# Moving shifted weight slots and the mixers' region from 64 to 128 bytes off their partner's remainder modulo 256

## The reference

```python
def conv_ffn(h, w_up, conv_w, conv_b, w_down):
    u = causal_dwconv(h @ w_up, conv_w, conv_b)
    g, val = u[..., :D_FF], u[..., D_FF:]
    return (jax.nn.gelu(g, approximate=True) * val) @ w_down

for layer in range(DEPTH):
    h = rms_norm(x, norm_mix_pre[layer])
    m = even_mixer(h, ...) if layer % 2 == 0 else odd_mixer(h, ...)
    x = x + rms_norm(m, norm_mix_post[layer])
    h = rms_norm(x, norm_ffn_pre[layer])
    x = x + rms_norm(conv_ffn(h, ...), norm_ffn_post[layer])
```

## Time and profile before

| | us |
|---|---|
| median of the runs | 1075.27 |
| profiled execution, whole | 1075.82 |
| its span, first to last instruction | 1074.0 |
| TensorE busy | 1064.7 |
| VectorE busy | 683.4 |
| ScalarE busy | 478.0 |
| GpSimd busy | 58.8 |

### The profile page before, as it was taken

The page is one execution under the profiler, slowest core; times in us unless marked ns, Lnnn a source line. Parts: engine busy times, 40 slices in busy tenths (PEclk is TensorE's granted clock), DMA queues, the critical chain, the costliest instruction groups (busy, mean ns, idle before and its releaser), DMA issues.

```text
span 1074.0 us, 14619 instructions
## 1 busy us (share of the span) xinstructions
PE 1064.7 (99%) x5782; PEld 899.0 (84%) x5782; DVE 683.4 (64%) x890; ACT 478.0 (45%) x694; POOL 58.8 (5%) x55
## 2 busy tenths in 40 slices
PE   9999999999999999999999999999999999999997
PEld 7876889988888888888899877998888888888886
DVE  6685875977767676522247777398776767663323
ACT  6454764644344343412236366465434434341321
POOL 0000002300000000001103000131000000000000
PEclk9999999999999999999999999999999999999999
DMA  7342141123222222222332623212323223234542
GB/s 239 118 118 70 49 143 63 70 79 110 87 97 99 85 110 82 105 97 80 109 117 63 178 72 119 97 61 79 113 84 101 95 84 111 84 112 92 144 118 79
DMA packets 39847, 107.71 MB, mean 100 GB/s; under 512 B 20721, under 2 KB 23537, under 8 KB 29169
## 3 DMA queue, kind: packets, MB, share of 16 engines
q1 hardware_dynamic: 39648, 106.94, 30.2%
q10 hardware_dynamic: 144, 0.01, 0.0%
HBM read 98.15 MB, written 2.10 MB: 93 GB/s over the span
## 4 chain that ended last, share of the span: by engine, by line
PE 96%; ACT 1%; DMA 1%; SPq 1%; issue 1%; DVE 0%; DVEq 0%; ACTq 0%
PE ps L1662 31%; PE ps L1664 30%; PE ps L1663 30%; PE ps L1827 1%; PE ps L1853 1%; PE ps L1838 1%; PE ps L2113 1%; PE ps L2102 1%; DMA w_raw<-in_odd_w_o 1%; PE ps L2129 1%; ACT prob L1093 0%; DMA w_raw<-in_even_w_in 0%; SPq L565 0%; PE ps L1735 0%; PE ps L1719 0%
## 5 line engine op out<-in xcount | busy, mean ns | idle before, releaser
L1662 PE MATMUL ps<-hx_hi,w_hi 128*128 128x512 f32 x812 | 320.3, 394 | 0.2 <-DVE w_lo L1163 0.2
L1664 PE MATMUL ps<-hx_hi,w_lo 128*128 128x512 f32 x812 | 316.5, 390 | 0.0
L1663 PE MATMUL ps<-hx_lo,w_hi 128*128 128x512 f32 x812 | 316.3, 390 | 0.0
L1140 DVE TENSOR_TENSOR w_lo<-w_raw,w_hi 128x2048 fp32r<-128x2048 f32 (+1 forms) x74 | 167.7, 2266 | 115.5 <-ACT w_hi L731 115.4
L731 ACT ACTIVATE w_hi<-w_raw 128x2048 fp32r<-128x2048 f32 (+1 forms) x76 | 142.1, 1871 | 127.0 <-DMA w_raw<-in_ffn_w_down 112.4
L1662 PEld LDWEIGHTS ps<-hx_hi,w_hi 128*128 128x128 f32 x812 | 152.5, 188 | 35.8 <-issue 4.6
L1664 PEld LDWEIGHTS ps<-hx_hi,w_lo 128*128 128x128 f32 x812 | 152.5, 188 | 32.0
L1663 PEld LDWEIGHTS ps<-hx_lo,w_hi 128*128 128x128 f32 x812 | 152.6, 188 | 30.8 <-issue 0.5
L1007 ACT ACTIVATE cg<-ug,vec 128x512 f32<-128x512 f32 x44 | 35.9, 816 | 136.5 <-DVE ug L1474 136.5
L1483 DVE SCALAR_TENSOR_TENSOR cg<-ug,vec,cg 128x511 f32<-128x511 f32 x88 | 65.8, 748 | 20.4 <-ACT cg L1007 20.4
L1019 ACT ACTIVATE g_hi<-cv 128x512 f32 (+1 forms) x44 | 27.8, 632 | 111.1 <-DVE cv L1492 111.1
(11 more groups left out here) (252 smaller groups left out, 1851.8 us busy)
## 6 DMA issues: line engine op xcount, KB each, us to landing
w_raw<-in_ffn_w_up SPq DMA_DIRECT2D x40, 1024.0 KB, 4.8
w_raw<-in_ffn_w_down SPq DMA_DIRECT2D x16, 1024.0 KB, 5.0
w_raw<-in_even_w_in SPq DMA_DIRECT2D x6, 1024.0 KB, 4.8
w_raw<-in_even_w_out SPq DMA_DIRECT2D x3, 1024.0 KB, 4.8
w_raw_s<-in_odd_w_qkv SPq DMA_DIRECT2D x3, 1024.0 KB, 4.8
w_raw<-in_odd_w_qkv SPq DMA_DIRECT2D x3, 1024.0 KB, 5.6
w_raw<-in_odd_w_o SPq DMA_DIRECT2D x3, 1024.0 KB, 5.0
rsw<-rp SPq DMA_DIRECT2D x40, 64.0 KB, 2.0
```

The source lines that it names most:

```text
L1140: dve.tensor_tensor(w_lo[s][:, 0:k], w_raw[s][:, 0:k], w_hi[s][:, 0:k], ALU.subtract).then_inc(w_lo_done, 1)
L1662: pe.matmul(dst, s_hi, r_hi, start=first, stop=False)
L1663: pe.matmul(dst, s_hi, r_lo, start=False, stop=False)
L1664: return pe.matmul(dst, s_lo, r_hi, start=False, stop=last)
```

## The change

The shift of slots goes from 320 to 128 bytes, and `big0` moves with it: both are then at 0 modulo 256 instead of 192. `w_hi_o` starts 128 bytes earlier than the place that it had in the region. `w_hi_e` moves from the place of `qT` to 128 bytes behind the start of the 21st block of 2048 bytes in the region, and the three tables of the rotary angles move from block 24 to block 12. No instruction, wait or DMA is added or taken away.

```diff
-SHIFT = 320
+SHIFT = 128
...
-    big0 = g0 + 320
+    big0 = g0 + SHIFT
...
-    ang, turns, angc = (at(n, [P, T], F32, big0 + (24 + i) * T * 4) for i, n in enumerate(("ang", "turns", "angc")))
+    ang, turns, angc = (at(n, [P, T], F32, big0 + (12 + i) * T * 4) for i, n in enumerate(("ang", "turns", "angc")))
...
         if i:
-            w_hi.append(at("w_hi_o", [P, UK, 2, P], F32R, big.at_))
+            w_hi.append(at("w_hi_o", [P, UK, 2, P], F32R, big.at_ - SHIFT))
...
-    w_hi.append(at("w_hi_e", [P, UK, 2, P], F32R, q_at))
+    w_hi.append(at("w_hi_e", [P, UK, 2, P], F32R, big0 + 20 * T * 4 + SHIFT))
```

## The result

The changed kernel is slower: a median of 1078.98 us over 6 runs (1078.52 to 1081.32), against 1075.36 over 6 runs of the kernel before on the same chip. The ratio is 1.0033, with a 95% interval of 1.0023 to 1.0044. Its profiled execution took 1078.68 us, 2.9 more than the one before, and so did its span. The forecast was 1070.8; what came is rival 2, "distance 128 is dearer".

A forecast was written before the change was run, and what follows sets the result against it. TensorE's matmul count times start-to-start distance bounds the kernel. 5.9 us gained, less 0.5 attention, 0.4 boundary and 0.5 restarts, leaves 4.5: 1071.3 for the profiled execution, 1070.8 for the median (own range 1069 to 1073; overall 1068.8 to 1077.3).

The forecast's parts named there:

- rival 2: 256-column matmuls: distance 128 is dearer, a third pace of 120.2 ns, +5.1 us, 1080.4; chance 0.15.
- The step that failed: Three-matmul products: distance makes the short pace possible, so 128, which no row had, was chosen for nearly all.
- the short pace: 256-column matmuls starting 113.3 ns apart instead of 117.8; about 350 of 1704 had it, worth 4.5 ns each.
- The sum: 1317 long-paced 256-column matmuls all take the short pace: 5.9 us gained, 4.5 left after deductions.
- The deductions for waits: Taken off the gain: 0.5 us where attention mixes with output projection, 0.4 at the boundary at 201 to 220.
- The 118.6 at distance 0: Upper parts at 0 and lower parts at 64, 688.82 to 690.48: 14 distances, read as the long pace.
- four longer ones: Stretches not shown with weights moving and hx 64 below, said to be long-paced like 587 to 597.
- Its threshold for a loss of 0.2%: Under rival 2, the kernel is slower by over 0.2% once the new pace exceeds about 118.8 ns.
- Rival 1: 256-column matmuls: restart timing, not addresses, chooses the pace; 1075.3 us, between 1073.7 and 1076.9; chance 0.35.
- Rival 3: 256-column matmuls: the collision vanishes, pace 109 ns as for plain fp32 transposes, -12 us, 1063.3; chance 0.06.
- the edits at nothing: 512-column matmuls (0.2 us either way), VectorE splits, slot transfers, moved angle tables and upper parts: all taken as 0.
- The sign given for rival 2: Stretches 201 to 220, 529 to 546, 568 to 583 and 587 to 597 would show starts 119 ns or more apart.

The follow-up runs named there:

- experiments 1 and 8: Small kernel of three-matmul products alone: first stationary-moving distance swept in 16-byte steps, then five distances with sixteen restarts each; at 128 bytes 118.7 or 120.0 ns a matmul.
- experiment 7: Distance 0 everywhere (no slot shift, mixers' region at g0) against the kernel before: 1079.45 us, ratio 1.0043, mean pace 119.85 ns.
- experiment 12: Against a kernel with slots at 76 and moving weights at 144, output projections' middle units take slots 76 above: 1071.88 us, ratio 0.9965 to the kernel before.
- The small kernel: Follow-up kernel without the network, only three-matmul products on operands loaded and split beforehand, 48 matmuls a setting; paces at 256 columns include 113.3, 117.8, 118.7 and 120.0 ns.
- experiment 2: Only the shifted slots go to distance 128, the rest as in the kernel before: 1076.89 us against 1075.71, ratio 1.0015.
- the second: Second sweep of the small kernel, in 4-byte steps: all distances of 512 columns, 256 columns around 64 above; no 512-column pace under 226.7 ns.

## Why the prediction was wrong

**The step that failed** is the one that the prediction called a choice: "distance is what makes the short pace possible", with 128 as "the farthest two remainders of 256 can be from 0". From three distances (0, 64 above, 64 below) it drew a rule in which 128 would be better than both. Between 64 and 128 there is no such slope: 113.3 and 117.8 at 64, 120.0 or 118.7 at 80, 118.7 at 96, 120.0 or 118.7 at 128 (experiments 1 and 8). The rows did hold the clue that such a rule needs at least a sign, short stretches far more often above than below, and the prediction read it as 128 "between the two sides". Placing a thing between two measured sides said nothing of it.

**The sum** had 1317 x 4.5 = 5.9 us as its gain. In its place the 1317 went from 117.8 and the 350 from 113.3 to a mean of 119.3, 3.9 us more. The deductions for waits (0.5 in the attention, 0.4 at the boundary) were about waits that a faster TensorE would find; a slower one lost existing waits instead, 0.77 and 0.45 us, shown above. A forecast of a loss needs that term as much as one of a gain. Two readings in the working were off as well. The 118.6 at distance 0 was a short sample of a mixture (experiment 7), so the price of distance 0, 120.0, was not known. And the trace before has two more stretches with the weights moving (31 to 41 and 107 to 115), not four longer ones; both are long-paced, as it says.

**Rival 2** had the mechanism, a third pace above 117.8 at each restart, and put it at 120.2 by the 2.4 ns of another width. Its paces were 120.0 and 118.7. Its threshold for a loss of 0.2%, a pace above 118.8, comes out at 118.4 by its own terms. It came out at 1080.4 because it took all matmuls at the upper one (0.9 ns too much on 1665, 1.5 us) and only 0.5 us for waits; 1078.98 was measured. Its chance of 0.15 was the fault: a distance of which no row exists deserved no better than even terms between dearer and cheaper. **Rival 1** was right that a restart picks the pace, and wrong that the address has no part (experiments 1, 7 and 8). **Rival 3** asked for 109 ns; no distance came below 113.3.

**Right**: the edits at nothing. The 512-column matmuls cost 0.2 us, inside the stated 0.2, those at distance 0 kept 226.7, and the splits, the DMAs and the moved tables changed nothing that the page shows. The 2470 against 2318 ns of the splits, which the prediction left open as a price of the address, is none: it comes from the two long ones beside GpSimd (experiment 12). The sign given for rival 2, stretches at 119 or more, is what about half of the matmuls in the changed kernel's long stretches show; the other half has 118.7.

**The Trainium skill** says in TensorE: Matmul & The Clock Gate, "Step-by-step: what each phase is for", that loading the next tile's weights takes no read bandwidth from the running matmul. The small kernel does not agree: with nothing else running, the start of the stationary operand alone moves the pace from 113.3 to 120.0 ns at 1.00 of the clock. Whether it is read bandwidth that the two reads share, or something else, no run shows: the runs tell of addresses and times only.

## What to carry to other kernels

When TensorE reloads its stationary operand for every matmul, the placement of that operand against the moving one is a parameter with a price, here up to 6.7 ns in 113 for each matmul of 256 columns. Sweep it in a small kernel, with several restarts for each value, before laying out memory: a value that shows the good pace once may only permit it (64, 8 of 16 restarts), and another may give it each time (76, 16 of 16). Then read it again in the whole kernel, since a stretch can get another pace there with none of its own addresses moved. Don't interpolate between distances, and keep the moving operand's start fixed while you vary the other.

## What the runs showed of the hardware

The pace of three-part products repeated after 256 bytes of distance in 47 of 48 settings, and it depends on the sign: in 16 restarts each, 64 above took 113.3 or 117.8 ns in turn and 64 below 117.8 always, while 0 took 120.0 and 128 took 118.7 or 120.0. In the whole kernel 64 below took 113.3 as well. A step of 4 bytes, from 76 to 80, took it from 113.3 to 118.7. At one distance, 76, the moving operand's start within 32 bytes moved the pace between 113.3 and 120.0. The pace can change at a restart with every address as it was (118.0 and 113.3 ns in experiment 2). Products of 512 columns had no better distance than 0, at 226.6 to 226.7 ns; others took up to 234 in the first sweep and 243 in the second. A split on VectorE that took 2.28 to 2.29 us took 2.83 and 3.38 when it began during an addition on GpSimd.
